# Taking TensorE's unread products out of the waits of a two-block transformer kernel

## The reference, cut to what matters

```python
h = h + rms_norm_2(m, mix_post_g[layer])                              # post0, post1
f = squared_relu_mlp(rms_norm_2(h, ffn_pre_g[layer]), w_ff1[layer], w_ff2[layer])
h = h + rms_norm_2(f, ffn_post_g[layer])                              # ffpost0, ffpost1

u = lax.conv_general_dilated(u, w_dw[:, None, :], ...) + b_dw         # conformer, 31 taps
u = jax.nn.silu(layer_norm(u, ln_g, ln_b))                            # the layer norm, ln_var
return u @ w_pw2 + b_pw2

q = (rms_norm_2(hn @ w_dq, q_norm_g) @ w_uq).reshape(b, s, N_HEADS, QK_HEAD_DIM)
v = (c_kv @ w_uv).reshape(b, s, N_HEADS, V_HEAD_DIM)                  # latent attention, 8 heads
```

## Time and profile before

| what | value |
|---|---|
| median of three runs | 1814.08 us (1810.33 to 1817.05) |
| the profiled execution's own time | 1813.4 us |
| its span, first to last instruction | 1811.6 us |
| TensorE busy | 1771.5 us (98%), 8104 products |
| VectorE, ScalarE, GpSimd busy | 54%, 34%, 11% |
| mean granted TensorE clock | 0.992 of full speed |
| DMA | 156.05 MB, 86 GB/s |

### The profile page before, as it was taken

The page is one execution under the profiler, slowest core; times in us unless marked ns, Lnnn a source line. Parts: engine busy times, 40 slices in busy tenths (PEclk is TensorE's granted clock), DMA queues, the critical chain, the costliest instruction groups (busy, mean ns, idle before and its releaser), DMA issues.

```text
span 1811.6 us, 21991 instructions
## 1 busy us (share of the span) xinstructions
PE 1771.5 (98%) x8104; PEld 1436.8 (79%) x8104; DVE 986.7 (54%) x1322; ACT 620.4 (34%) x909; POOL 194.3 (11%) x175
## 2 busy tenths in 40 slices
PE   6999999999999999999999999999999999999998
PEld 5777888888888888877888888877767788888886
DVE  4666446673565489985642344346675564234432
ACT  4345234442343342244422222234253433112221
POOL 2100021110011200101110011000000111001111
PEclk9999899999999999999999999999999999999999
DMA  5212023333233222312233233221310223223321
GB/s 181 88 47 70 13 92 113 94 106 115 84 102 100 75 93 93 105 59 94 79 96 104 93 93 102 95 82 58 92 37 1 94 82 104 93 93 95 103 82 46
DMA packets 43844, 156.05 MB, mean 86 GB/s; under 512 B 4864, under 2 KB 4992, under 8 KB 43776
## 3 DMA queue, kind: packets, MB, share of 16 engines
q1 hardware_dynamic: 43632, 154.19, 26.8%
q10 hardware_dynamic: 144, 0.92, 0.1%
HBM read 153.00 MB, written 2.10 MB: 86 GB/s over the span
## 4 chain that ended last, share of the span: by engine, by line
PE 94%; DVE 4%; ACT 1%; issue 1%; DMA 0%; SPq 0%; ACTq 0%; DVEq 0%
PE bank L1023 27%; PE bank L1024 27%; PE bank L1025 27%; PE bank L1168 1%; PE bank L1174 1%; PE bank L1169 1%; PE bank L1244 1%; DVE w_lo L1695 1%; PE bank L1064 1%; PE bank L1273 1%; PE bank L1110 1%; PE bank L1628 1%; PE bank L1098 0%; PE bank L1058 0%; PE bank L1259 0%
## 5 line engine op out<-in xcount | busy, mean ns | idle before, releaser
L1695 DVE TENSOR_TENSOR w_lo<-w_raw,w_hi 128x1024 fp32r<-128x1024 f32 x283 | 364.9, 1292 | 314.3 <-ACT w_hi L613 191.5
L1023 PE MATMUL bank<-a_hi,w_hi 128*128 128x512 f32 x1156 | 460.3, 398 | 20.1 <-DVE w_lo L1695 17.4
L1024 PE MATMUL bank<-a_lo,w_hi 128*128 128x512 f32 x1156 | 455.7, 394 | 0.0
L1025 PE MATMUL bank<-a_hi,w_lo 128*128 128x512 f32 x1156 | 453.5, 392 | 0.0
L1023 PEld LDWEIGHTS bank<-a_hi,w_hi 128*128 128x128 f32 x1156 | 218.7, 189 | 74.6 <-issue 15.1
L1023 PE MATMUL bank<-g_hi,w_hi 128*128 128x512 f32 x688 | 270.1, 393 | 0.0
L1024 PE MATMUL bank<-g_lo,w_hi 128*128 128x512 f32 x688 | 270.0, 392 | 0.0
L1025 PE MATMUL bank<-g_hi,w_lo 128*128 128x512 f32 x688 | 267.6, 389 | 0.0
L1025 PEld LDWEIGHTS bank<-a_hi,w_lo 128*128 128x128 f32 x1156 | 218.4, 189 | 49.1
L1024 PEld LDWEIGHTS bank<-a_lo,w_hi 128*128 128x128 f32 x1156 | 218.9, 189 | 46.2 <-issue 1.0
L613 ACT ACTIVATE w_hi<-w_raw 128x1024 fp32r<-128x1024 f32 x167 | 174.4, 1050 | 196.5 <-PE bank L1025 191.3
(11 more groups left out here) (288 smaller groups left out, 1987.4 us busy)
## 6 DMA issues: line engine op xcount, KB each, us to landing
w_raw<-in_stream SPq DMA_DIRECT2D x283, 512.0 KB, 3.5
h<-in_xT SPq DMA_DIRECT2D x8, 256.0 KB, 6.4
out<-h SPq DMA_DIRECT2D x8, 256.0 KB, 2.1
cst_b<-in_consts SPq DMA_DIRECT2D x1, 896.0 KB, 9.8
cst_b<-in_consts ACTq DMA_DIRECT2D x1, 896.0 KB, 4.5
cols<-in_vectors SPq DMA_DIRECT2D x1, 289.0 KB, 2.8
cst<-in_consts SPq DMA_DIRECT2D x1, 257.0 KB, 8.2
w_al<-in_w_alpha SPq DMA_DIRECT2D x1, 128.0 KB, 9.8
```

Of the source, the lines that this page charges most:

```text
L1023: pe.matmul(out, w0, x0, start=start, stop=False, skip_group_check=loose)
L1024: pe.matmul(out, w0, x1, start=False, stop=False, skip_group_check=loose)
L1025: return pe.matmul(out, w1, x0, start=False, stop=stop, skip_group_check=loose)
L1695: dve.tensor_tensor(w_lo[slot][:, :], w_raw[slot][:, :], f(w_hi[slot][:, :]), ALU.subtract)\
```

## The change

All calls of `run_idle` go, and the function with them. Nothing else is edited: no wait, no other instruction. There are 30 such products: five at each of `post0`, `ffpost0` and `post1` (one in `stat`, four in `spread`), ten in the layer norm, four in front of the latent heads and one at the last residual add. The norm `ffpost1` keeps the `h_part` products that stand in the same places, since those are read.

```diff
-            def run_idle(free, count, width=SEQ):
-
-                for _ in range(count):
-                    pe.matmul(bank[free][:, 0:width], cst[:, IDENT:IDENT + P], cst[:, 0:width], start=True, stop=True)
...
                 if name == "ffpost1":
                     pe.wait_ge(out_read, TILE0["ff2b1"])
                     h_part(2, 0, 384)
-                elif "post" in name:
-                    run_idle(6, 1, 384)
                 pe.wait_ge(sq_ready, SQ0[name] + n)
...
                 if name == "ffpost1":
                     h_part(4, 0, 384)
-                elif "post" in name:
-                    run_idle(6, 1, 384)
                 pe.wait_ge(r_tok_ready, STAT_NO[name] + 1)
...
                 last.then_inc(spread_done, 1)
-                if "post" in name and name != "ffpost1":
-                    run_idle(6, 3)
...
             pe.wait_ge(out_read, TILE0["pw2"])
-            run_idle(0, 2)
             pe.wait_ge(mean_add, KD - 2)
...
             last.then_inc(mean_done, 1)
-            run_idle(0, 2)
-            run_idle(0, 2)
...
             pe.wait_ge(ln_pairs, 1)
             ln_sum(0, True, False)
-            run_idle(0, 1, 192)
             pe.wait_ge(ln_pairs, 2)
             ln_sum(2, False, False)
-            run_idle(0, 1)
             pe.wait_ge(ln_folded, 1)
             ln_sum(4, False, True).then_inc(stat_done, 1)
-            run_idle(0, 1, 256)
             spread("ln_var")
-            run_idle(0, 1)
             tiles("pw2", 8, a_hi, a_lo, "conv")
...
             pe.wait_ge(out_read, TILE0["uv"] + 1)
-            run_idle(0, 4)
             pe.wait_ge(rope_split, 10)
...
             h_part(6, 0, SEQ)
-            run_idle(6, 1)
             for k in (2, 4, 6):
```

## The result

The changed kernel takes 1823.09 us, the median of five runs (1821.82 to 1830.46), against 1814.43 us of the kernel before (1810.33 to 1817.05). The ratio is 1.0057, with a 95% interval of 1.0032 to 1.0081. It is slower by 0.6%, inside the range that was forecast and near its upper end: +8.7 us where +4.5 was the sum. The profiled execution took 1822.15 us.

A forecast was written before the change was run, and what follows sets the result against it. TensorE, busy 98% of the span, was taken to bound the kernel. Terms +0.3 (layer norm), +3.6 (residual norms), +0.2 (heads) and +0.4 (last add) sum to +4.5 us: 1818 us, range 1811 to 1825.

The forecast's parts named there:

- Rival 1: Residual norms: the clock holds through the narrow products, -1.2 us instead of +3.6; total 1811 to 1813 us; chance 0.17.
- Rival 3: Residual norms: full products are slow only for a moment, sum about +2 us, total 1815 to 1816 us; chance 0.13.
- Rival 2: After each norm the clock stays low for 6.4 us of full work, +3.6 us each; total 1830 us; chance 0.12.
- more than 4 us of full products at 0.50: Sign in the profile after that the clock stays low longer than the forecast's up to 3 us behind the residual norms.
- the bound of +2.0: Upper bound for each residual norm, whose forecast was +1.2 us and whose lower bound was -0.4.
- the first full products behind a residual norm: Full products run at 0.50 for up to 3.2 us, costing 1.6 us, of which three quarters was charged: +1.2 us each norm.
- `spread` at half speed: Residual norms: if the clock falls before line 1110, `spread` costs 0.8 us more; half was charged, +0.4 us each norm.
- The 0.4 us won in the queue: Residual norms: without unread products 0.16 us is won before line 1110 and 0.26 before line 1168, -0.4 us each.
- The layer norm: 1.3 us won in the queue, 1.6 us lost by `pw2` at 0.50: +0.3 us, bounds -1.3 and +1.9.
- The heads: In front of the latent heads TensorE idles 5 us and the scores run at half speed: +0.2 us, bounds 0 and +1.7.
- VectorE's cover: Latent heads: VectorE, busy with low parts until about 1334.4, hides nearly all of the scores' 1.6 us delay.
- The last residual add: Line 1681's last product would take nearly 2.0 us instead of 1.14; half of 0.9 charged: +0.4 us, bounds 0 and +1.7.

The follow-up runs named there:

- narrow_fill: Kernel before, with one-column unread products at the three residual norms, four for each of 384 columns and twelve for the three of 512: 1825.66 us, ratio 1.0055.
- stat_fill: Kernel before, with only the two 384-column unread products in front of `spread` kept at the residual norms, the three of 512 columns removed: 1816.20 us, ratio 1.0016.
- ln_wide: Kernel before, with 384 instead of 192 columns between the layer norm's sums and one more unread product of 256 behind the second sum: 1815.07 us, ratio 0.9999.
- tail_fill: Kernel before, with only the three 512-column unread products behind `spread` kept at the residual norms, the two of 384 columns removed: 1821.01 us, ratio 1.0023.
- fitted_again: Second measurement of the kernel before with unread products resized to the waits at layer norm and residual norms, none in front of the mean: 1817.28 us, ratio 0.9998.
- fitted: Kernel before with unread products resized to the waits at layer norm and residual norms, none in front of the mean: 1811.80 us, ratio 0.9992.
- split_fill: Kernel before, with 128-column unread products at the residual norms, three for each of 384 columns and twelve for the three of 512: 1815.14 us, ratio 1.0007.

## Why the prediction was right, and where its sizes were off

**The direction and the mechanism.** Fewer products, more time. The clock fell at the norms, at the layer norm and in front of the heads, as forecast, and not at the last residual add; the sum of places is the slowdown. Rival 1 (the clock holds) is rejected by the changed kernel's profile and by `narrow_fill`. Rival 3 (slow only for a moment) is rejected: the full products were slow for 4.4 to 5.5 us at the norms. Rival 2 (low for 6.4 us of full work) is not met either, but its sign, more than 4 us of full products at 0.50, came at all three norms. With 7.9 us the norms lie between the 3.6 of the forecast and the 10.8 of rival 2, and two of the three lie above the bound of +2.0 that I gave them. The time stayed inside the range since the other places stayed 3.6 us below their upper bounds. The direction was earned, the size only in part.

**The mis-sized term: the first full products behind a residual norm.** The forecast was 1.2 us a norm, three quarters of half of 3.2 us. In the trace the full products run at half speed for 5.0 us after `post0` (857.08 to 862.1), 5.5 after `ffpost0` (1221.8 to 1227.3) and 4.4 after `post1` (1448.2 to 1452.6). From the first full product to the end of the stretch these norms take 2.1, 2.2 and 1.75 us more than in the kernel before. That is a little less than half of the slow stretch (2.5, 2.8 and 2.2), so a few tenths are won back, which I had ruled out; where is not traced. The 3.2 us came from the two places of the kernel before where full work followed a fall, and both happened to take 3.2. Taking three quarters of it was a choice in the wrong direction. I argued that an early fall lets part of the low stretch pass before full work begins. It did not help: the clock fell 5.2, 4.7 and 2.4 us before the first full product, and stayed low for 5.0, 5.5 and 4.4 us behind it. What sets this length, 3.2 us in those two cases and up to 5.5 here, stays open.

**`spread` at half speed.** I charged half of 0.8 us. The clock was low through all of it at `post0` and `ffpost0` (2.09 us for 0.97 in the chain) and high through nearly all of it at `post1` (1.16 us by the timeline, 1.13 before). The first full product starts 7.8 us after the norm's first product instead of 6.9 at `post0`, 7.7 instead of 6.8 at `ffpost0`, and 6.8 in both at `post1`: +1.0, +0.9 and 0. Together with the term above that is the +3.05, +3.1 and +1.75 measured.

**The 0.4 us won in the queue.** It did not come. I had compared the ends of unread products in the chain of waits with the starts of the next weight loads, and a product's shown end lies behind the start of the next one (full products last 0.39 us here and start every 0.23). By the starts of products, line 1110 begins 3.41 us after line 1089 in the kernel before and 3.43 in the changed one (line 1101), and line 1168 begins 6.86 us after it both in the kernel before and in `stat_fill`, which has nothing behind `spread`. So at a residual norm the unread products delay nothing as long as the clock holds. The stretch of 26.24 us in `stat_fill` against 26.44 proves no gain either, since the kernel before's own code took 26.29 in `ln_wide`.

**The layer norm.** Forecast +0.3, measured +1.0, within the bounds. Of the 1.3 us to be won, 0.9 came. Centring starts 157.64 us after `pre0` instead of 158.45, 0.8 us sooner. The first product of `pw2` starts 0.9 us sooner, so that `spread` and the unread product behind it gave 0.1 us and not 0.6: `spread` starts 0.3 us sooner after the last sums and takes 2.08 us instead of 1.92. Against that, the full products were at half speed for 4.3 us, not 3.2, and from the first of them to `post0` it takes 1.9 us more, where I had charged 1.6. The comparison is with a profile in which the kernel before lost its clock here too. In three of its code's five profiles it kept it (214.0 us), and against those the loss is 2.6 to 2.9 us.

**The heads.** Forecast +0.2, measured +0.7, and 0.6 and 0.3 in the two other profiles without the products. The first scores and the last maximum in the changed kernel's timeline, TensorE's row and VectorE's in two views:

```profile
1334.60 0.77 PE L1609 MATMUL bank<-k_nope,q_nope 128*128 128x128 f32 x2 [5.03 <-issue]
```

```profile
1341.35 0.69 DVE L2213 TENSOR_REDUCE small<-bank 128x1 f32<-128x512 f32 x1 [0.83 <-PE bank L1613]
```

The clock came back 5.4 us after the first score, not 3.2, so the last maximum waited 0.83 us. VectorE's cover was real: the last record of the scores starts 6.3 us after the first instead of 3.75, and of these 2.6 us it hid 1.9.

**The last residual add.** Forecast +0.4, measured nothing, in the three profiles without the product. The clock was 1.00 until 1816 in the changed kernel, and its chain ends as before:

```profile
1810.96 3.96 DVE m L2258 x6
...
1814.97 1.14 PE bank L1661 x2
```

In these profiles the unread product at the end brings nothing.

**What the sum left out.** The same code loses its clock in one execution and keeps it in the next. In the profiled execution the gap before `uk` took 1.5 us less by chance, which hid part of a loss of 9.6. By the prediction's own sign (a difference outside the places of the change) this would count against it, as would the +0.6 at the start, but both lie within what these stretches vary by from profile to profile.

## What to carry to other kernels

A product that nobody reads can be worth its time when it fills a wait of TensorE in front of full work, and it must have some width: 128-column products held the clock here, one-column products did not although TensorE never paused. Price a fall by how long the full work behind it runs slow (3.2 to 5.5 us in the two kernels, of which two fifths to a half was lost), not by the length of the gap. If the clock falls all the same, the unread products themselves run at half speed and delay the next one that is read, as in `tail_fill`. Put no such product where it ends after the wait it is to fill, as in front of the mean here. And compare stretches between two products in the timeline: they mostly repeat to 0.3 us or better where whole runs scatter by 5 us and more. Whether a delay is real is read from the starts of products, not from their ends.

## What the hardware showed that I had not expected

- The same code falls or holds. The gap before `uk` kept the clock in 5 of 11 profiles (17.5 us against 19.0), the kernel before's layer norm in 3 of 5 (214.0 against 215.9 or 216.1), and in `stat_fill` the same norm code held twice and fell once in one execution. What decides it stays open.
- In two of eleven profiles TensorE's products were slower in a long stretch at a granted clock of 1.00. In 200 us of the first block, in the kernel before:

```profile
420.00:620.00 200.00, 200.00 (x875) 164.11 (x874) 111.50 (x126) 72.78 (x92) 24.34 (x16) 1.00 0.30 95
```

and in `ln_wide`, with the same code there:

```profile
420.00:620.00 200.00, 200.00 (x859) 161.98 (x858) 108.10 (x122) 69.46 (x87) 20.28 (x13) 1.00 0.30 93
```

  859 products instead of 875, 0.233 us apart instead of 0.229, in all 4.65 us from `ffn` to `pre0`. It came in `fitted_again` too, whose profiled execution took 1817.49 us against 1811.54 in `fitted`: 4.6 of these 6 us lie in that stretch. That the other runs of 1816 us and more have the same cause fits by size and is not shown. What causes it stays open.
- In the heads two profiles (`tail_fill`, `split_fill`) have 141.7 us instead of 140.2 with the kernel before's code there, each with a fall of the clock there (at 1394.3 and 1388.7 us).
